# Heads of state-space, attention and first feed-forward stage: split work and norm work in another order

## The reference

```python
for layer in range(2):
    h = h + 0.5 * swiglu(rms_norm(h, g), w_gate, w_up, w_down)     # feed-forward 0, 2
    hn = rms_norm(h, mix_norm[layer])
    h = h + (s5_mixer if layer == 0 else moba_mixer)(hn, ...)      # state space, attention
    h = h + 0.5 * swiglu(rms_norm(h, g), w_gate, w_up, w_down)     # feed-forward 1, 3
```

## Time and profile before

| | us |
|---|---|
| median of 3 runs | 1956.85 |
| profiled execution | 1958.92 |
| its span, first to last instruction | 1957.1 |
| PE busy in it | 1762.7 (90%) |
| DVE busy | 1449.0 (74%) |
| ACT busy | 618.0 (32%) |
| mean granted TensorE clock | 0.965 |

### The profile page before, as it was taken

One profiled execution on the slowest core, in us unless ns is written; L12 is line 12 of the kernel. 1 busy time (PEld: TensorE's weight loads), 2 busy tenths in 40 slices (PEclk: granted clock), 3 DMA queues, 4 the chain that ended last, 5 costly groups with the idle time before them and its releaser, 6 DMA issues.

```text
span 1957.1 us, 25151 instructions
## 1 busy us (share of the span) xinstructions
PE 1762.7 (90%) x9580; PEld 1330.9 (68%) x9580; DVE 1449.0 (74%) x2725; ACT 618.0 (32%) x810; POOL 409.9 (21%) x366
## 2 busy tenths in 40 slices
PE   6999988777787777789999898999999999999999
PEld 4788843333332333338999766899989998779998
DVE  7887789888888888768886698665575556867554
ACT  2235320110001100006443312545454444456452
POOL 0001145444544545420000197000000000000000
PEclk9999999988989989999999899999999999999999
DMA  9853699999999999984554422545545554534453
GB/s 394 317 199 130 235 399 417 422 421 422 421 422 421 422 416 418 412 364 177 182 200 172 151 90 84 194 168 186 193 162 193 193 182 140 172 133 153 181 188 118
DMA packets 63854, 502.13 MB, mean 257 GB/s; under 512 B 7200, under 2 KB 7456, under 8 KB 11296
## 3 DMA queue, kind: packets, MB, share of 16 engines
q0 software_dynamic: 37008, 268.98, 33.2%
q1 hardware_dynamic: 25920, 230.45, 32.1%
q10 hardware_dynamic: 848, 1.69, 0.2%
HBM read 500.04 MB, written 1.05 MB: 256 GB/s over the span
## 4 chain that ended last, share of the span: by engine, by line
PE 62%; DMA 16%; DVE 15%; POOL 3%; ACT 2%; issue 2%; SPq 0%; DVEq 0%; ACTq 0%; POOLq 0%
PE PB L921 24%; DMA arena<-in_uv,eidx 12%; PE PB L932 12%; PE PB L903 7%; DMA ring<-in_uv,eidx 3%; DVE arena L1698 3%; PE PB L644 2%; PE PB L1078 2%; PE PB L715 2%; PE PB L597 1%; PE PB L701 1%; PE PB L812 1%; DVE gu_lo L1261 1%; PE PB L994 1%; PE PB L947 1%
## 5 line engine op out<-in xcount | busy, mean ns | idle before, releaser
L903 PE MATMUL PB<-arena 128*128 128x512 f32 x604 | 300.2, 654 | 98.8 <-DVE arena L1720 98.8
L921 PE MATMUL PB<-h_hi,gu_hi 128*128 128x256 f32 x1344 | 377.0, 280 | 0.5 <-DVE gu_lo L1782 0.5
L921 PE MATMUL PB<-h_hi,gu_lo 128*128 128x256 f32 x1344 | 376.9, 280 | 0.0
L921 PE MATMUL PB<-h_lo,gu_hi 128*128 128x256 f32 x1344 | 375.8, 280 | 0.0
L903 PEld LDWEIGHTS PB<-arena 128*128 128x128 f32 x604 | 122.8, 209 | 275.4 <-issue 144.7
L2633 POOL DMA_INDIRECT arena<-in_uv,eidx x193 | 227.1, 1176 | 315.2 <-PE PB L903 209.3
L1698 DVE CUSTOM_DVE_ANT_0 arena<-arena,XN 128x1024 f32<-128x1024 f32 x187 | 223.2, 1223 | 64.2 <-DMA arena<-in_uv,eidx 64.1
L921 PEld LDWEIGHTS PB<-h_hi,gu_hi 128*128 128x128 f32 x1344 | 254.1, 189 | 4.4 <-DVE gu_lo L1782 1.1
L921 PEld LDWEIGHTS PB<-h_lo,gu_hi 128*128 128x128 f32 x1344 | 252.0, 187 | 3.1
L921 PEld LDWEIGHTS PB<-h_hi,gu_lo 128*128 128x128 f32 x1344 | 252.8, 188 | 0.0
L1792 DVE TENSOR_TENSOR act_gs<-PB,XN 128x256 f32<-128x256 f32 x88 | 37.4, 425 | 242.9 <-PE PB L921 241.8
(11 more groups left out here) (446 smaller groups left out, 3046.2 us busy)
## 6 DMA issues: line engine op xcount, KB each, us to landing
ring<-in_ffn SPq DMA_DIRECT2D x88, 1536.0 KB, 6.4
arena<-in_ada SPq DMA_DIRECT2D x24, 768.0 KB, 8.7
ring<-in_qkv SPq DMA_DIRECT2D x12, 1024.0 KB, 4.8
ring<-in_zg SPq DMA_DIRECT2D x8, 1024.0 KB, 5.5
ring<-in_s5b SPq DMA_DIRECT2D x8, 1024.0 KB, 4.8
ring<-in_ada SPq DMA_DIRECT2D x4, 1536.0 KB, 16.0
ring<-in_up SPq DMA_DIRECT2D x4, 1024.0 KB, 4.8
ring<-in_wo SPq DMA_DIRECT2D x4, 1024.0 KB, 7.3
```

What stands on the lines that cost most here:

```text
L903: mm = pe.matmul(PB[2 + 2 * t + h][:, :], lhsT=diag(n), rhs=uv[n % UVB][:, 1, h * 512:(h + 1) * 512], start=False, stop=False, skip_group_ ...
L921: mm = pe.matmul(PB[j % 2][:, b * T:(b + 1) * T], lhsT=w[:, j % 2, o:o + P], rhs=h[:, k, :], start=(k == 0 and m == 0), stop=(k == DC - 1 ...
```

## The change

Four parts.

1. First feed-forward head. Unit 0 gets split buffers of its own (`f0_hi`, `f0_lo`). ACT copies it in group 57 of the gather, and squares row tile 0 of X there; DVE subtracts in group 59, between the dots and the diagonals. After the gather the copy, the square and the subtraction are gone from the head, and the root comes after all four pairs on both engines. ACT waits for the gather's end (`uv_used`) only ahead of unit 1.
2. State-space head. `trail("s5in", 1)` moves from ahead of the residual to behind the whole head.
3. State-space input. PE uses four banks in turn instead of two, and waits for the chunk four before. POOL builds the first decay table when three chunks of u are kept.
4. Attention head. `trail("qkv", 1)` is cut in two halves, which stand between the pairs; the norm's sums and root move behind all pairs. PE no longer waits for the unit's low part ahead of pair 2, since the first half stands ahead of pair 2's `h_lo` on DVE.

```diff
@@ PE: state-space input
-                                mm = pe.matmul(PB[c][:, 0:T], lhsT=w[:, w_part % 2, o:o + P], rhs=h[:, k, :],
+                                mm = pe.matmul(PB[(2 * i + c) % 4][:, 0:T], lhsT=w[:, w_part % 2, o:o + P],
+                                               rhs=h[:, k, :], start=(k == 0 and m == 0),
...
-            split_chunks("s5in", 4, lambda c: pe.wait_ge(u_done, c - 1) if c >= 2 else None)
+            split_chunks("s5in", 4, lambda c: pe.wait_ge(u_done, c - 3) if c >= 4 else None)
@@ PE: feed-forward, first unit; attention
+                            hi, lo = (gu_hi[:, 0, :], gu_lo[:, 0, :]) if f else (f0_hi[:, :], f0_lo[:, :])
...
-                pe.wait_ge(pw_lo_done, w_part + 1)
+                if (m, q) != (0, 2):
+                    pe.wait_ge(pw_lo_done, w_part + 1)
@@ DVE: gather, routed(g)
+                if g == NGRP - 5:
+                    dve.wait_ge(gu_hi_done, 1)
+                    v.tensor_tensor(f0_lo[:, :], ring[:, ffn_base[0] % NS, 0:2 * D], f0_hi[:, :].bitcast(F32),
+                                    ALU.subtract).then_inc(gu_lo_done, 1)
@@ DVE: head of feed-forward 0
-                    split_gate_up(0)
                     split_pairs(n, 0, 1)
                     norm_sums(n)
-                    split_pairs(n, 2)
+                    split_pairs(n, 2, 3)
                     norm_root(n)
-                    split_pairs(n, 3)
                     diagonals()
@@ DVE: end of feed-forward 0 and 2, heads behind them
                     trail("s5in", 0)
-                    trail("s5in", 1)
...
                     trail("qkv", 0)
-                    trail("qkv", 1)
...
             head(N_S5)
+            trail("s5in", 1)
...
-            head(N_MOBA)
+            split_pairs(N_MOBA, 0, 1)
+            trail_half(0)
+            split_pairs(N_MOBA, 2)
+            trail_half(1)
+            split_pairs(N_MOBA, 3)
+            norm_sums(N_MOBA)
+            norm_root(N_MOBA)
@@ ACT: gather, and head of feed-forward 0
+                if g == NGRP - 7:
+                    act.wait_ge(w_here[ffn_base[0] % NS], 16 * (ffn_base[0] // NS + 1))
+                    s.copy(f0_hi[:, :], ring[:, ffn_base[0] % NS, 0:2 * D]).then_inc(gu_hi_done, 1)
+                    act.wait_ge(x_done, 6)
+                    tell(s.activation(XN[:, 0, :], X[:, 0, :], ACT.Square, accum_out=stat[:, 0:1]), sq_act)
...
                 if f == 0:
+                    tell(s.activation(stat[:, 14:15], ones[:, 0:1], ACT.Sqrt), act_link)
+                    split_h(n, 3)
                     act.wait_ge(uv_used, TT * NSLOT)
-                    lead_next_block(0)
-                norm(n)
-                split_h(n, 0 if f else None)
+                else:
+                    norm(n)
+                    split_h(n, 0)
                 lead_gate_up(1)
-                if f == 0:
-                    norm_root(n)
@@ ACT: attention; POOL: decay table
-            split_h(N_MOBA)
+            split_h(N_MOBA, 3)
...
-                    pool.wait_ge(x_done, 12)
+                    pool.wait_ge(u_done, 3)
```

More of the change, by code:

```diff
@@ L223, in up_lo @@
             return ring_r[:, 2 * (i - 2) + c, 2 * D:3 * D]
+        f0_hi = split_at("f0_hi", [P, 2 * D], arena_at + 4 * 8192)
+        f0_lo = split_at("f0_lo", [P, 2 * D], arena_at + 4 * 10240)
         def wo_lo(i):
@@ L628, in split_chunks @@
                             for m, (w, h) in enumerate(products):
-                                mm = pe.matmul(PB[c][:, 0:T], lhsT=w[:, w_part % 2, o:o + P], rhs=h[:, k, :],
-                                               start=(k == 0 and m == 0), stop=(k == DC - 1 and m == 2))
+                                mm = pe.matmul(PB[(2 * i + c) % 4][:, 0:T], lhsT=w[:, w_part % 2, o:o + P],
+                                               rhs=h[:, k, :], start=(k == 0 and m == 0),
+                                               stop=(k == DC - 1 and m == 2))
                         mm.then_inc(half_done if c == 0 else unit_done, 1)
@@ L945, in gate_up_first @@
                             o = (b * DC + k) * P
-                            for m, (w, h) in enumerate(products):
-                                mm = pe.matmul(PB[0][:, b * T:(b + 1) * T], lhsT=w[:, 0, o:o + P],
+                            hi, lo = (gu_hi[:, 0, :], gu_lo[:, 0, :]) if f else (f0_hi[:, :], f0_lo[:, :])
+                            for m, (w, h) in enumerate(((hi, h_hi), (hi, h_lo), (lo, h_hi))):
+                                mm = pe.matmul(PB[0][:, b * T:(b + 1) * T], lhsT=w[:, o:o + P],
                                                rhs=h[:, k, :], start=False, stop=(k == DC - 1 and m == 2),
@@ L1905, in _ @@
                     dve.wait_ge(unit_done, UNIT[("s5in", c // 2)] + 1)
-                tell(v.tensor_tensor(uT[:, c, :], PB[c % 2][:, 0:T], rrow, ALU.mult), u_done)
+                tell(v.tensor_tensor(uT[:, c, :], PB[c % 4][:, 0:T], rrow, ALU.mult), u_done)
             dve.wait_ge(tab_ready, 2)
@@ L1995, in _, with trail_half @@
             ffn(2)
-            head(N_MOBA)
+            def trail_half(h):
+                p, u = SPLIT[("qkv", 1)], UNIT[("qkv", 1)] % NS
+                dve.wait_ge(pw_hi_done, p + 1)
+                cs = slice(h * D, (h + 1) * D)
+                ins = v.tensor_tensor(gu_lo[:, p % 2, cs], ring[:, u, cs], gu_hi[:, p % 2, cs].bitcast(F32), ALU.subtract)
+                if h:
+                    ins.then_inc(pw_lo_done, 1)
+            split_pairs(N_MOBA, 0, 1)
[5 more added lines that the diff above has]
+            norm_root(N_MOBA)
             def keep_second_tile(m):
```

## The result

The changed kernel takes 1945.62 us (median of 4 runs, 1943.52 to 1945.95), the kernel before 1957.61 beside it (4 runs, 1956.72 to 1959.37). The ratio is 0.9934, with a 95% interval of 0.9922 to 0.9947. The forecast was 1943.2 with a range of 1941 to 1948. The profiled execution took 1945.49 and its span 1943.7, so 13.4 us less than the span before; the prediction had 13.7 and 1943.4.

A forecast was written before the change was run, and what follows sets the result against it. PE bounds the feed-forward stages, transfers the gather, DVE's chain the state-space head; 7.2 (state-space) + 2.7 (attention) + 3.8 (first feed-forward) = 13.7 us off the median 1956.85 gives 1943.2, range 1941 to 1948.

The forecast's parts named there:

- rival 1: Clock falls in the heads after all; 2.55 us lost in state-space head, total 1945.8, at worst 1947.5; chance 20%.
- a stretch of 0.50 remains in the state-space head: Sign of a wrong forecast: granted clock still at 0.50 (1.2 GHz) in the state-space head.
- The other signs: Attention's first product 4.8 us after residual's start; feed-forward second unit 11.5 after last gathered product; gather still ends at 885.
- Subtraction, 2.2: State-space head: one of two subtractions leaves the place ahead of the residual, which starts 2.2 us earlier.
- Stall of the scaling, 1.6: State-space head: POOL's table no longer starts with the norm, so the scaling takes 0.17 us, not 1.74.
- PE's first unit, 2.55: State-space head: PE's first unit takes 5.99 us in place of 8.54, if the clock stays up.
- Banks, 0.8: State-space input: four banks take away the wait for the banks, the remaining 0.8 of the head's 7.2 us.
- Attention head, 2.7: Attention head: PE starts at 1642.7 in place of 1645.44, 2.7 us earlier, with the moved work all hidden.
- First feed-forward head, 3.8: First feed-forward head: first scaling 2.9 us earlier and DVE's 0.93 wait for the root gone, 3.8 together.
- rival 3: Heads' end set by load of unit 1, POOL meeting DVE or late root; 1 to 1.6 each, 1946; chance 10%.
- Gather, 0: Gather: added subtraction delays group 59's diagonals, but PE doesn't wait; bounds 0 to 2.3 us, taken as 0.
- Decay table's new place, 0: State-space input: table (1.89 us) and DVE's subtraction of unit 3 don't meet; cost taken 0.

The follow-up runs named there:

- early table: Changed kernel with the first decay table started behind the residual again (x_done 12); 1947.80 us, second unit 16.59 us after the low part's start (15.03 without).
- the attention head alone: Kernel before with only the edits of the attention head; 1953.94 us, attention interval 6.90 us (9.71 before).
- the subtraction alone: Kernel before with only the subtraction of state-space unit 1 moved behind the norm's diagonals; 1959.84 us, state-space interval 18.91 us (21.19 before).
- two banks: Changed kernel with two banks in place of four for the state-space input projection; 1946.25 us, second unit 16.33 us after the low part's start.
- by 11.5 in the second: Changed kernel timed again on the same chip as the kernel with both idle times filled; median 1946.60 us, kernel before 1958.1, ratio 0.9940.

## Why the prediction was right, and where it was off

The measured 1945.62 lies in the range of 1941 to 1948, but outside 1941.5 to 1945, which the forecast kept for itself, and nearest to the 1945.8 of rival 1. One of the signs named for a wrong forecast, "a stretch of 0.50 remains in the state-space head", came: the second unit started 12.81 us after the residual's first instruction (1087.66 - 1074.85), not 11.8. The other signs came as forecast: 4.69 us in attention (4.8), 11.3 from the last gathered product to the second unit of the first feed-forward (11.5), and the gather's end at 884.35. Term by term:

- *Subtraction, 2.2:* 2.28 alone (21.19 - 18.91). The prediction puts PE's last products (1080.6) at 0.1 us into the second subtraction; it is 0.8. The residual's start doesn't hang on it.
- *Stall of the scaling, 1.6:* 1.56 alone, between the kernels with and without the early table. The scaling is long only beside the table. The copy also runs beside DVE's sum ahead of the scaling, so which of the two lengthens the copy is not shown.
- *PE's first unit, 2.55:* **this step failed.** "Now PE has work in the state-space head until 1083.3 and idles some 1.7 us" was right to 0.03 us; that this keeps the clock was wrong. It fell, for 3.4 us and not for the whole unit, so 1.1 of the 2.55 came (8.54 to 7.46). This is rival 1 in its mild form: it had 20% and 1945.8 for the time. That the idle time is what drops the clock there is shown by filling it: with a fill the first unit took 5.82 or 5.83 in five of five profiles, with none 7.28 to 7.30 in four of four. That the 1.1 is the change's is not shown: in the unedited head the unit took 8.38 and 8.29, but once 7.29 (the attention head alone), and of two kernels with 3.29 us of idle time one had 8.31 (the subtraction alone) and one 7.29 (the early table).
- *Banks, 0.8:* 1.30 with this alone undone. The forecast took it as a remainder. The four together are 2.28 + 1.56 + 1.08 + 1.30 = 6.2, and 6.16 were measured. Of these 5.1 belong to edits; against the unedited head with 20.09 the changed one gains 5.08 (15.01).
- *Attention head, 2.7:* 2.81, alone as in the whole. PE's idle time there is 1.26 us, and the clock held. At most 0.14 of it is the clock's fall in the kernel before: without that fall the old head took 9.57 (the kernel with the one subtraction moved).
- *First feed-forward head, 3.8:* 4.03, alone 4.0. The transfer of unit 1 had been put as landing at 892.1, and ACT's copy starts at 891.08 after a wait of 0.54. It ends at 892.99, and DVE comes to its subtraction only at 893.29, so the load did not set this term, with 0.3 us to spare. With two banks the same load was later (ACT waited 0.93): DVE waited 0.24 for the copy, and the head took 12.22. This is the late load that rival 3 named, at a price of 0.2.
- *Gather, 0:* at most 0.3. PE was busy from 840 to 850 as before, and the dip of the transfers there was made good.
- *Decay table's new place, 0:* no meeting. It runs from 1092.27 to 1094.2, the subtraction of unit 3 starts at 1095.67.

The heads together gave 4.03 + 6.16 + 2.81 = 13.0, less 0.5 between the marks: 12.5. How much of that 0.5 is the change's is open: most of it lies in one stretch, from the first product of the scans to the attention head, which took 519.55 us in the changed kernel and from 518.2 to 519.7 in all thirteen profiles (519.1 to 519.3 in the four with the old state-space input). The medians moved by 12.0 in the first comparison and by 11.5 in the second.

The forecast for the profiled execution, 1945.2, was met (1945.49), partly by luck: the state-space head fell short by 1.0 and the stretches between by 0.5, the gather happened to be 0.9 shorter, and two heads gave 0.3 more than forecast. The other loose step was the one from the profile to the median: the profiled execution of before stood 2.07 above the median shown, and the sum was taken off the median all the same. With the second set of runs of before at 1957.61 the forecast would have been 1943.9. Of the remaining 1.7 the clock in the state-space head has 1.1 or more, by the fill.

## What to carry to other kernels

Work that ends just before a dependent chain and isn't needed first belongs behind it, and such moves add up: the feed-forward and the attention head, edited alone, gave what they give in the whole. In the head of a stage look at PE's idle time as well as at the chain; where the granted clock falls behind it, a few products of zeros into a free bank, placed where PE would wait anyway, cost nothing and gave 1.1 us here. Undo one edit at a time and read a stage's interval between two marks, when the whole time moves by several us from run to run in a stage that the edit doesn't touch; and look at the granted clock in both profiles before a difference is put down to the edit.

## What the runs showed of the hardware

- In the changed kernel's state-space head the granted clock fell to 0.50 behind 1.73 us of idle PE (in three of three profiles with this idle time, and in the one with 3.29), and six products of zeros or fifteen fp32 transposes in it kept it at 1.00 (five of five). Behind 1.26 us in the attention head it held in every profile read there.
- The idle time alone doesn't tell whether the clock falls or for how long. In the kernel with the one subtraction moved it held in the attention head through idle times of 2.25 and 1.73 us, where in the kernel before it fell behind 2.24 ahead of the transposes. In the state-space head 1.73 and 3.29 us gave first units of 7.30 and 7.29 (changed kernel, early table), and 3.29 gave 8.31 with the one subtraction moved. In the kernel before (8.38) the clock had already fallen during the transposes, ahead of the last idle time.
- At the gather's end the same stage came with either clock, with idle times of 2.8 us ahead of both: 2.79 with 5.42 behind it (the attention head alone), 2.81 with 7.11 (the one subtraction moved); the gather is that of the kernel before in both. The residual then starts 1.9 or 2.7 us behind the last gelu. Which of the two comes is not settled.
- A two-element instruction on DVE took 1.73 us beside a copy of 128x2048 on POOL, in place of 0.17, and the copy 2.94 in place of 1.90, in all five profiles in which they met. The Trainium skill (GPSIMD Engine Reference, section 1, Specifications) says that the two engines share their interfaces to SBUF, with contention for DVE instructions in a 2-port mode or with two SBUF inputs. The trace agrees that they hold each other up; which of these cases the instruction is, no run here shows.
